# One accumulation buffer in DRAM instead of two for the routed experts of a hybrid mixer and MoE block

## The reference

```python
h2 = rmsnorm(x, g_ffn).reshape(b * s, d)
shared = swiglu(h2, s_gate, s_up, s_down)
routed = routed_experts(h2, w_router, router_bias, e_gate, e_up, e_down)
x = x + (shared + routed).reshape(b, s, d)
return rmsnorm(x, g_final)
```

## Time and profile before

| | |
|---|---|
| Three executions | 2767.49, 2770.04, 2771.02 us (median 2770.04) |
| The profiled execution | 2770.64 us, span in the trace 2768.7 us |
| Mean granted clock of PE | 0.981 |
| Busy share of the span | PE 96%, DVE 65%, POOL 48%, ACT 44% |
| DMA traffic | 523.53 MB, mean 189 GB/s |

### The profile page before, as it was taken

How to read it: one execution, slowest core, us unless ns; L and a number is a source line. 1 busy time by engine, 2 the same in 40 slices (tenths; PEclk the granted TensorE clock), 3 DMA queues, 4 the chain that set the end, 5 groups by cost and what they waited for, 6 DMA issues and landing times.

```text
span 2768.7 us, 51226 instructions
## 1 busy us (share of the span) xinstructions
PE 2654.3 (96%) x11902; PEld 2168.9 (78%) x11903; DVE 1804.8 (65%) x2519; ACT 1214.3 (44%) x1738; POOL 1321.1 (48%) x1116
## 2 busy tenths in 40 slices
PE   7999999999999999739999999999999999999996
PEld 6888888788887888627888888888888888888875
DVE  5544555555555655547877877777877777777576
ACT  3233323232332223215656655565665555556432
POOL 3000002200221013367777877777877777777611
PEclk9999999999999999959999999999999999999998
DMA  8223433442334234428888988888988888888764
GB/s 310 96 94 114 137 97 101 130 143 98 101 127 144 92 107 129 140 87 235 268 252 247 291 264 240 231 241 243 285 263 241 248 233 237 230 233 239 214 208 175
DMA packets 169917, 523.53 MB, mean 189 GB/s; under 512 B 37716, under 2 KB 43528, under 8 KB 169872
## 3 DMA queue, kind: packets, MB, share of 16 engines
q1 hardware_dynamic: 95776, 344.42, 35.0%
q0 software_dynamic: 65888, 164.39, 25.1%
q10 hardware_dynamic: 8208, 14.16, 1.5%
HBM read 434.97 MB, written 119.18 MB: 200 GB/s over the span
## 4 chain that ended last, share of the span: by engine, by line
PE 51%; DVE 2%; issue 1%; ACTq 1%; ACT 0%; POOL 0%; DMA 0%; DVEq 0%; POOLq 0%
PE ps_gu L1471 11%; PE ps_gu L1472 11%; PE ps_gu L1473 11%; PE ps_y L1473 6%; PE ps_y L1471 6%; PE ps_y L1472 5%; PE ps_h L1518 1%; ACTq L1626 1%; DVE xl L1669 0%; DVE xt L1658 0%; ACT xh L1548 0%; DVE y L1731 0%; DMA xs<-h_dram,gidx 0%; DVEq L1729 0%; DVE y L1728 0%
## 5 line engine op out<-in xcount | busy, mean ns | idle before, releaser
L1412 POOL DMA_INDIRECT xs<-h_dram,gidx x656 | 830.1, 1265 | 200.4 <-issue 199.5
L1471 PE MATMUL ps_gu<-expert_hi,xl 128*128 (+1 forms) x1392 | 565.6, 406 | 19.0 <-DVE xl L1669 18.5
L1472 PE MATMUL ps_gu<-expert_lo,xh 128*128 (+1 forms) x1392 | 550.3, 395 | 0.0
L1473 PE MATMUL ps_gu<-expert_hi,xh 128*128 (+1 forms) x1392 | 550.1, 395 | 0.0
L1653 DVE TENSOR_TENSOR expert_lo<-expert_raw,expert_hi 128x1024 f32 (+1 forms) x390 | 459.8, 1221 | 81.5 <-ACT expert_hi L1548 62.7
L917 DVE TENSOR_TENSOR ul<-raw,uh 128x1024 fp32r<-128x1024 f32 x186 | 227.9, 1225 | 401.8 <-ACT uh L741 379.3
L1548 ACT ACTIVATE expert_hi<-expert_raw 128x1024 f32 (+1 forms) x390 | 391.0, 1053 | 69.2 <-PEq L1522 42.3
L93 POOL TENSOR_SCALAR rstd<-mean 128x1 f32<-128x1 f32 x49 | 12.1, 247 | 844.5 <-ACT junk L760 829.3
L504 PE MATMUL ps_t<-hh,ul 128*128 128x512 f32 x1024 | 401.6, 392 | 3.1 <-DVE wgl L1146 3.1
L505 PE MATMUL ps_t<-hl,uh 128*128 128x512 f32 x1024 | 399.1, 390 | 0.0
L506 PE MATMUL ps_t<-hh,uh 128*128 128x512 f32 x1024 | 399.1, 390 | 0.0
(11 more groups left out here) (263 smaller groups left out, 3936.2 us busy)
## 6 DMA issues: line engine op xcount, KB each, us to landing
expert_raw<-experts SPq DMA_DIRECT2D x396, 512.0 KB
raw<-units SPq DMA_DIRECT2D x192, 512.0 KB
xs<-h_dram,gidx POOLq DMA_INDIRECT x656
h_dram<-h ACTq DMA_DIRECT2D x17, 512.0 KB
acc_odd<-h POOLq DMA_DIRECT2D x17, 512.0 KB, 15.7
acc<-x SPq DMA_DIRECT2D x4, 2048.0 KB, 8.0
expert_raw<-acc_odd SPq DMA_DIRECT2D x16, 512.0 KB, 4.6
expert_raw<-x POOLq DMA_DIRECT2D x14, 512.0 KB, 3.7
```

Source lines behind the costliest of these rows:

```text
L1412: nc.gpsimd.indirect_dma_start(xs[s][:, g * DQ:(g + 1) * DQ], None, h2_quarters, bass.IndirectOffsetOnAxis(ap=gidx[s][:, g:g + 1], axis=0) ...
L1471: nc.tensor.matmul(out_, sl, vh, start=first, stop=False)
L1472: nc.tensor.matmul(out_, sh, vl, start=False, stop=False)
L1473: return nc.tensor.matmul(out_, sh, vh, start=False, stop=last)
```

## The change

The tensor `acc_odd` goes, with its 17 zeroing DMAs, its loads at the end and the DVE addition (with its drain) that joined the two. All scatters add to `acc`. Because neighbouring blocks can now add to the same row, POOL waits ahead of each scatter for the one just before it as well.

```diff
@@ build
-    acc_odd = nc.dram_tensor("acc_odd", [S + P, D], F32, kind="Internal").ap()
@@ route
-        SETS = 16 * (10 + S // P + 1)
+        SETS = 16 * 10
@@ route, POOL
             x_norm(TT, TT)
             x_load(TT + 1, 1)
-            for i in range(0, S + P, P):
-                pool.dma_start(acc_odd[i:i + P, :], h2[:, :]).then_inc(dram_set, 16)
@@ mixture
-        tile_odd = [raw[:, 2 + k, :] for k in range(TILES)]
@@ mixture, SP: load_tile
-                sp.dma_start(tile_acc[k][:, :], acc_tiles[0][t]).then_inc(tile_in[k], 16)
-                sp.dma_start(tile_odd[k], acc_tiles[1][t]).then_inc(tile_in[k], 16)
+                sp.dma_start(tile_acc[k][:, :], acc_tiles[t]).then_inc(tile_in[k], 16)
@@ mixture, POOL: scatter and the loop
-                    accs[s], bass.IndirectOffsetOnAxis(ap=sidx[s][:, 0:1], axis=0), y[s][:, :], None,
+                    acc, bass.IndirectOffsetOnAxis(ap=sidx[s][:, 0:1], axis=0), y[s][:, :], None,
...
                     pool.wait_ge(y_ready, i * 2 + (d + 2))
                     pool.wait_ge(y_out[1 - s], i * 16 + 16)
+                    pool.wait_ge(y_out[s], i * 16 + 16 * d)
                     carry(pool, marks)
                     scatter(1 - s)
@@ mixture, DVE: add_tile
-                dve.wait_ge(tile_in[k], (t // TILES + 1) * 32)
-                V.tensor_tensor(tile_acc[k][:, :], tile_acc[k][:, :], tile_odd[k], ALU.add)
-                dve.drain()
+                dve.wait_ge(tile_in[k], (t // TILES + 1) * 16)
```

More of the change, by code:

```diff
@@ L116, in build, with route @@
         piece_in = [sem(f"piece_in{p}") for p in range(PIECES)]
-        route(nc, sem, marks, table, slots, expert_raw, piece_in, experts, acc, acc_odd, h2_dram, lists, x, units,
+        route(nc, sem, marks, table, slots, expert_raw, piece_in, experts, acc, h2_dram, lists, x, units,
               wgroup, pool_scale, conv_w, b_gate, g_mix, g_ffn, w_router, router_bias, inv_count, ident, tri, iotas)
-        mixture(nc, sem, marks, table, slots, expert_raw, piece_in, (acc, acc_odd), h2_dram, experts, ident,
+        mixture(nc, sem, marks, table, slots, expert_raw, piece_in, acc, h2_dram, experts, ident,
                 g_final, out)
-def route(nc, sem, marks, table, slots, expert_raw, piece_in, experts, acc, acc_odd, h2_dram, lists, x, units,
+def route(nc, sem, marks, table, slots, expert_raw, piece_in, experts, acc, h2_dram, lists, x, units,
           wgroup, pool_scale, conv_w, b_gate, g_mix, g_ffn, w_router, router_bias, inv_count, ident_in, tri_in, iotas):
@@ L1282, in _, with mixture @@
             dve.drain()
-def mixture(nc, sem, marks, table, slots, raw, piece_in, accs, h2_dram, experts, ident_in, g_final, out):
-    acc_tiles = [a.rearrange("(n p) d -> n p d", p=P) for a in accs]
+def mixture(nc, sem, marks, table, slots, raw, piece_in, acc, h2_dram, experts, ident_in, g_final, out):
+    acc_tiles = acc.rearrange("(n p) d -> n p d", p=P)
     out_tiles = out.rearrange("(n p) d -> n p d", p=P)
```

## The result

The kernel after takes 2850.05 us in the median (2842.81 to 2858.11, 4 runs), the kernel before on the same chip 2769.18 us. The ratio is 1.0293, 95% interval 1.0271 to 1.0315: 81 us slower. The forecast of 2765.9 us and its range were wrong. Rival B, with a chance of 0.09 and a price of 2846 us, is what happened. The profiled execution has a span of 2856.4 us; it is the slowest of the four, so the sums from its trace are measured against 87.7 us (2856.4 - 2768.7) and not against 81.

What follows compares the result with a forecast made beforehand. PE was taken to bound token mixing and the routed loop, with slack only in the last stage. Zeroing 0, PE's waits -2.8, the end -1.3, the wait 0: -4.1 us, from 2770.04 to 2765.9 us, range 2762.0 to 2770.5.

Steps and rivals of the forecast that it cites:

- Rival B: Loop over routed blocks: the added wait ahead of each scatter becomes the bound, +80 us, about 2846 us; chance 0.09.
- Zeroing removed: Token mixing: dropping the 17 zeroing DMAs gains 0, as PE's own work hides them.
- PE's waits in the shared blocks: Shared blocks: without the joining addition PE no longer waits for DVE's `hid` over 11 steps, -2.8 us.
- the end: Behind PE's last block: without the joining addition the store of tile 12 comes earlier, passes stay, -1.3 us.
- C: Shared blocks: PE's waits come from ACT's DMA issue, so only the 1.3 us remain, 2768.7 us; chance 0.13.
- D: Last stage: halved tile traffic also shortens POOL's gaps in three passes, 3 us more, 2762.9 us; chance 0.10.
- Landing is between 5.4 + 0.5 = 5.9 and 6.6 + 1.8 = 8.4 us, and I take 6.5: Routed loop: time from a scatter's start to its landing, as last byte plus time to semaphore; 6.5 us taken.
- The cost in the loop is 0.: Routed loop: scatters land before POOL returns to the next one, so the added wait costs 0.
- the upper bound: Routed loop: landing at most 8.4 us, which would hold back only the shortest pairs, by 0.2 us.
- one place: First scatter of the routed loop, under a full load of weights: costs POOL 0 to 0.8 us once, taken as 0.
- the margin: Routed loop: landing of 6.5 us leaves 1.7 us against POOL's shortest return of 8.16, 2.1 against the mean of 8.59.

Runs made afterwards that it cites:

- the end alone: Kernel before without the second buffer's tile loads and the joining addition, odd blocks' sum left out, no wait added: 2766.28 us, ratio 0.9985.
- the wait alone: Kernel before with both buffers kept and only the added wait of POOL for the scatter just before: 2855.92 us against 2771.09, ratio 1.0301.
- the landing probe: Kernel after, with POOL waiting for each scatter's landing directly behind it, ahead of the four gathers: 3445.84 us, one run.
- the mid probe: Kernel after, with POOL also waiting for each scatter's landing after two of the four gathers behind it: 3075.46 us, one run.
- less traffic: Kernel after, with only the left half of each piece of the expert weights loaded: 2767.30 us, ratio 0.9984.

## Why the prediction was wrong

**Zeroing removed: 0.** Right. PE is busy for 1110.34 us in the token mixing, 0.07 more than before.

**PE's waits in the shared blocks: -2.8, and the end: -1.3.** Right, both to 0.1 us: 13 steps of 8.587 us with none longer, 4.2 us in place of 5.5, and passes that stay. The two long steps at the start of the stage come with the added wait and not from these terms: the end alone has none. The end alone measured -4.8 for -4.1, within its interval (-1.7 to -6.4 us). Rivals C and D fall.

**"Landing is between 5.4 + 0.5 = 5.9 and 6.6 + 1.8 = 8.4 us, and I take 6.5", and so "The cost in the loop is 0."** This is the step that failed, in three places: the wait alone costs 85 us and not 0.

First, the value. A full scatter that nothing disturbs lands after 7.4 us by the landing probe. The last byte was put at 5.4 us by the rate in the earlier trace rows and the receipt at about 1.1, and one of the two was too short; the probe gives only their sum. The estimate from the Trainium skill, "DMA: Bandwidth & Descriptors", section "Anatomy of one DMA — SWDGE (gpsimd) path", with 2.0 us for the receipt, was 7.4 us and agrees with the measured 7.42, as a sum; the 5.4 us in it are my own reading.

Second, and this decided, the upper bound. Both bounds came from one scatter, that of 1901.37, in a stretch where the DMA engines went quiet. A bound from one event holds for that event. With the weights' load beside it the landing is 9.3 us in the mid probe, and 11 us where the kernel after is pressed, at 1910.79. The trace of before had such a case in it, the first scatter with 8.9 us of slow phase, and I put it down as one place. But the loads of weights come with each of the 64 experts, and 63 of 157 gaps begin with an expert's last block, beside such a load. The prediction named this itself as what would make it wrong, a landing that depends on its load more than one steady stretch shows. The stage's DMA share of 0.85, given for rival B, was the sign that a quiet stretch is the exception.

Third, the margin. I compared the landing with POOL's return, 8.16 us in the shortest case and 8.59 in the mean, as if POOL could average long against short landings. A wait can't be averaged so. What it can win back is POOL's own reserve, 8.59 - 7.2 = 1.4 us a block, and a landing of 10 to 11 us makes a gap of 10.4 to 11.4 us, 1.8 to 2.8 us too long for the block in which it falls, so a part is lost for good before the next one comes.

**Rival B.** Its mechanism and place were right. It was priced with a period of 9.1 us, and the measured mean is 9.13; 2846 us against 2850.05. That closeness is in part luck: the 9.1 came from an assumed mean landing of 9.0 us for all blocks, where the long landings are those of some 63 blocks, and a part of the time went with ACT's stalls, which no rival had. Its condition, a mean landing above 8.4 us, was too strict: with landings of 7.3 and 9.3 to 11 us the mean need not pass 8.4 for the loss to start. What was wrong was the chance of 0.09.

**Why the landing is long.** Shown are two things that lengthen it. One is the weights' load beside the scatter: 9.3 against 7.25 us in the mid probe, and with half of the loads' bytes gone the whole loss is gone. The other is the addition: 7.42 against 4.61 us for a landing that nothing disturbs, and without it POOL's and DVE's waits of the chain above are gone, and half of the loss with them. Shown not to matter are two gathers behind the scatter and the sharing of one tensor.

**What stays open.** In the kernel after ACT stands still a few times for what the trace can't name, as ahead of `sg` here, in the waits between 1300 and 2690 us:

```profile
ACT sg L1568 <- remote: 34.4, 8, 7.5
...
ACT hth L1544 <- remote: 21.6, 7, 4.2
```

PE's five longest steps (12.6 to 15.4 us) each have such a stall in them, and with the steps behind them they hold 34 of the 95 us; all eleven steps with such a stall hold 45, counted the same way. In the kernel before, `sg` and `hth` have one each, 8.4 us together, and with half of the weights' traffic there is one, 4.7 us. The stalls do not simply follow the waits for landings under load. The mid probe waits for one in every block and has none. The kernel that overwrites, where POOL waits for a scatter once, has more of them than the kernel after:

```profile
ACT sg L1568 <- remote: 58.3, 15, 6.0
...
ACT hth L1544 <- remote: 27.7, 8, 4.6
...
POOL acc L1416 <- DMA acc<-y,sidx: 2.9, 1, 2.9
```

Its PE steps lie 56 us above 8.59 in all, and 43 of these are in the steps with such a stall and those right behind. So the half of the loss that is left there does not pass through late gathers. What makes ACT stand still is not known, and no experiment here separates it. Loading of instructions by DMA, as far as the trace shows it, is not it: the queues for that move nothing in the kernel after between 1277 and 2719 us, and all 17 stalls lie in there. That the added wait, under the full traffic of the weights, costs the whole loss is shown by two runs (the wait alone, less traffic). The way by late gathers is shown for a part of it; how much goes by ACT's stalls stays open.

## What to carry to other kernels

A wait for a DMA's landing has to be costed with the landing under the heaviest traffic that recurs in the loop, not with one that can be seen well because the queues are quiet. The engine that waits can win back only its own reserve, here 8.6 - 7.2 = 1.4 us a block, so the long landings decide and not the mean. And a buffer that only serves to keep two transfers apart is cheap as long as its upkeep (zeroing, loads, one addition) lies beside other work: here it cost 4 to 5 us and saved 85.

## What the runs showed of the hardware

An indirect scatter that adds lands more slowly than one that overwrites, with 128 rows of 4 KB: 7.42 against 4.61 us from the start of POOL's instruction to the first instruction behind the wait. It also holds the queues longer for the same bytes (a share of 0.84 at 235 GB/s against 0.70 at 241). With fewer than 36 rows the adding one still takes 5.3 to 6.0 us.

A stall costs PE more than its own length. Three stretches of the kernel after, columns as for the stages:

```profile
1505.00:1518.00 13.00, 9.69 (x43) 1.00 0.70 176
1518.00:1530.00 12.00, 11.16 (x43) 0.86 0.75 211
1530.00:1545.00 15.00, 15.00 (x67) 1.00 0.88 273
```

PE stood still for 3.3 us in the first; in the second the granted clock is 0.86 in the mean, so part of it ran at 1.2 in place of 2.4 GHz, and in the third it is 1.00 again. The step behind the long one was 10.49 us instead of 8.59. The 19 stalls of 0.3 to 1.3 us cost 0.34 us each in the step behind them.
